# Attention order planned per engine, its output kept turned, w_o prepared early, and head loads moved to GpSimd's queue

## The reference

```
h = rms(x, g_pre_mix);  z = h @ w_in  -> q | k | v | f | B | C | u
logit(t, s) = q_t.k_s/8 + sum_{s<j<=t} log sigmoid(f_j + b_f),  s <= t;  attn = softmax(logit) @ v
conv = B * causal_conv3(C * u)
mix  = concat(rms(attn, g_attn_out), rms(conv, g_conv_out)) @ w_o
x    = x + rms(mix, g_post_mix)
y    = x + rms(relu(rms(x, g_pre_mlp) @ w_up)^2 @ w_down, g_post_mlp)
```

## Time and profile before

| | us |
|---|---|
| median of 3 runs (lowest, highest) | 2739.94 (2737.48, 2744.5) |
| the profiled execution's own time | 2737.44 |
| its span | 2735.8 |

### The profile page before, as it was taken

One profiled execution on the slowest core, in us unless ns is written; L12 is line 12 of the kernel. 1 busy time (PEld: TensorE's weight loads), 2 busy tenths in 40 slices (PEclk: granted clock), 3 DMA queues, 4 the chain that ended last, 5 costly groups with the idle time before them and its releaser, 6 DMA issues.

```text
span 2735.8 us, 41595 instructions
## 1 busy us (share of the span) xinstructions
PE 2664.9 (97%) x14966; PEld 2405.3 (88%) x14966; DVE 1515.6 (55%) x2603; ACT 1126.6 (41%) x2099; POOL 1300.7 (48%) x884
## 2 busy tenths in 40 slices
PE   8999999998999999999999999899999999999997
PEld 8999999897888888888889989889999988999996
DVE  5233344247888887765344344665556564556554
ACT  3201301107777877555333332534333344333433
POOL 3233334220101006553477776766556677566654
PEclk9999999999999999999999999999999999999999
DMA  6643534574565443568444546421211272212213
GB/s 199 199 123 110 175 108 142 189 199 103 124 150 122 100 102 117 167 183 244 143 168 163 196 169 225 170 74 64 77 61 61 85 277 96 73 61 66 72 61 108
DMA packets 294353, 364.26 MB, mean 133 GB/s; under 512 B 37576, under 2 KB 245392, under 8 KB 290128
## 3 DMA queue, kind: packets, MB, share of 16 engines
q1 hardware_dynamic: 257152, 316.15, 37.7%
q0 software_dynamic: 11808, 26.74, 3.1%
q10 hardware_dynamic: 25264, 19.66, 2.1%
HBM read 264.30 MB, written 97.94 MB: 132 GB/s over the span
## 4 chain that ended last, share of the span: by engine, by line
PE 46%; DVE 2%; POOL 1%; DMA 1%; issue 1%; ACT 0%; SPq 0%; DVEq 0%; POOLq 0%; ACTq 0%
PE dn_bank L3006 17%; PE up_bank L2982 15%; PE dn_bank L2962 7%; PE up_bank L2937 7%; DMA m_raw_up<-in_w_up 1%; DVE m_raw_up L2758 1%; POOL m_y L2517 1%; POOL m_w_up L2466 1%; DVE m_t L2758 0%; SPq L2342 0%; ACT m_junk L2659 0%; DVE m_y L2863 0%; DMA m_x<-scratch_x 0%; POOL m_u L2509 0%; DVE m_y L2817 0%
## 5 line engine op out<-in xcount | busy, mean ns | idle before, releaser
L3006 PE MATMUL dn_bank<-m_w_dn,m_u 128*128 128x512 f32 x2304 | 531.0, 391 | 5.4 <-ACT m_y L2692 4.3
L3006 PEld LDWEIGHTS dn_bank<-m_w_dn,m_u 128*128 128x128 f32 x2304 | 432.7, 188 | 96.0 <-ACT m_y L2692 4.0
L2982 PE MATMUL up_bank<-m_h,m_w_up 128*128 128x384 f32 x2688 | 476.1, 337 | 8.7 <-DVE m_stage L2772 4.5
L2982 PEld LDWEIGHTS up_bank<-m_h,m_w_up 128*128 128x128 f32 x2688 | 470.1, 189 | 12.7 <-issue 5.1
L2819 DVE TENSOR_TENSOR m_y<-dn_bank,m_y 128x1024 f32<-128x1024 f32 x168 | 205.7, 1224 | 270.4 <-PE dn_bank L3006 270.4
L508 POOL TENSOR_TENSOR w_lo<-w_raw,w_hi 128x1024 fp32r<-128x1024 f32 x72 | 176.0, 2448 | 342.3 <-DVE w_hi L722 342.3
L2509 POOL TENSOR_TENSOR m_u<-m_stage,m_u 128x384 fp32r<-128x384 f32 x128 | 141.5, 1128 | 281.7 <-ACT m_u L2648 281.7
L2466 POOL TENSOR_TENSOR m_w_up<-m_raw_up,m_w_up 128x512 fp32r<-128x512 f32 x128 | 192.2, 1521 | 65.2 <-ACT m_w_up L2616 65.2
L938 PE MATMUL proj<-ha_hi,w_hi 128*128 128x384 f32 (+1 forms) x640 | 212.1, 331 | 0.0
L1446 DVE TENSOR_TENSOR p_lo<-t_bank,p_hi 128x512 fp32r<-128x512 f32 (+1 forms) x336 | 197.9, 599 | 25.2 <-ACT p_hi L1393 24.6
L938 PE MATMUL proj<-ha_hi,w_lo 128*128 128x384 f32 (+1 forms) x640 | 210.0, 328 | 0.0
(11 more groups left out here) (304 smaller groups left out, 5674.4 us busy)
## 6 DMA issues: line engine op xcount, KB each, us to landing
m_raw_up<-in_w_up SPq DMA_DIRECT2D x48, 1024.0 KB, 5.4
m_raw_dn<-in_w_down SPq DMA_DIRECT2D x47, 1024.0 KB, 4.9
w_raw<-in_w_in SPq DMA_DIRECT2D x72, 512.0 KB, 4.1
scratch_h_pairs<-m_pieces POOLq DMA_DIRECT2D x12, 1792.0 KB, 8.2
m_h<-scratch_h_pairs SPq DMA_DIRECT2D x14, 1536.0 KB, 10.8
nck<-scratch_ncum SPq DMA_DIRECT2D x8, 1312.0 KB, 19.2
scratch_v_hl<-vhl SPq DMA_DIRECT2D x20, 512.0 KB, 2.7
q_hi<-scratch_q_hi SPq DMA_DIRECT2D x16, 528.0 KB, 7.3
```

The lines of the kernel that those rows point to most:

```text
L2982: mm = pe.matmul(out, w_up[:, j, wp, k, :], hidden_rows(g, j, hp, k), start=(k == 0 and p == 0), stop=(k == KH - 1 and p == 2))
L3006: mm = pe.matmul(bank[:, cols], part, wd[:, wp, b, cols], start=(b == 0 and p == 0), stop=(b == 1 and p == len(passes) - 1))
```

## The change

- **Order.** `attention_steps` lists the steps of all 40 groups (8 heads; order 0, EXTRA, 1, 2, 3). `attention_order` plays them through with a cost and a delay for each step and gives every engine a queue of its own, unrolled. Among steps that could start at the same time TensorE prefers T, then S, then V; VectorE T, S; ScalarE T, M, O. The plan knows the waits among TensorE, VectorE and ScalarE (banks, score sets, p buffers). It has no DMA in it and no GpSimd.
- **Turned output.** Step N, `n_bank` and the output's transposes go; there are two `o_bank`. ScalarE copies the two halves of the bank to the same 64 partitions (two instructions), GpSimd adds them (64x512) and multiplies with `scales`. SyncE stores to `attn_t`, which keeps queries in columns. There are two `o_t` buffers (`A_BUFS` = 2), and ScalarE's copy of group k waits for the store of group k-2.
- **Totals.** `scales` needs the reciprocals along the columns. VectorE, before the first `p_lo` of a group, takes the reciprocal and transposes a [128, 32] tile in 32x32 blocks; SyncE stores it in four small DMAs (two for EXTRA) to `rtotal`, waits for them, and loads the line back, broadcast to 64 partitions.
- **w_o.** Eight pieces of 128 rows, one every third group from group 5 on: SyncE loads the piece, GpSimd scales it by the gain, rounds it, takes the rest, SyncE stores both to DRAM. The gains are no longer applied to a and c. After the products of head 6, GpSimd's queue loads `w_hi` and `w_lo` (8 MB).
- **Loads.** The ten loads of a head stand on GpSimd's queue, behind the close of group 3 of head h-2 and ahead of the close of group 0 of head h-1.
- **Mix.** a comes turned, so `scale_rows`, `turn` and VectorE's part of the split go. ScalarE copies a and c to hi (`firsts`), GpSimd squares and sums both and makes both rests; two 1-column matmuls.

```diff
+    def cost(engine, x):
+        if engine == "pe":
+            if x.kind == "S":
+                return 2 * (x.width / 2.4 + 13) + (107 if x.last else 0), 320
+            if x.kind == "T":
+                return 109 * (x.width // P), 260
+            return (2 * len(x.blocks) * 107 if x.group.extra else 2 * (x.width / 2.4 + 13)), 300
+        if engine == "dve":
+            return x.width / 0.96 + 67 + (400 if x.kind == "T" and x.first else 0), 150
...
+    while True:
+        chosen = None
+        for engine, kinds in FIRST_CHOICE.items():
+            for rank, kind in enumerate(kinds):
...
+                    start = max(free[engine], ready(engine, x))
+                    if start < math.inf and (chosen is None or start < chosen[0] or (start == chosen[0] and engine == chosen[1] and rank < chosen[2])):
+                        chosen = start, engine, rank, x
...
         def _(sp):
+            for q in groups:
...
+                store_scales(q)
+                load_scales(q)
+                k, at = divmod(q.k - W_FIRST, W_EVERY)
+                if 0 <= k < KB and at == 0:
+                    load_piece(k)
+                if 0 <= k < KB and at == 2:
+                    store_piece(k)
+                if q.k:
+                    store(groups[q.k - 1])
...
         def _(pool):
+            fetch(1)
+            for q in groups:
...
+                close(q)
+                k, at = divmod(q.k - W_FIRST, W_EVERY)
+                if 0 <= k < KB and at == 1:
+                    split_piece(k)
+                if q.g == GROUP_ORDER[-1] and q.head + 2 <= HEADS:
+                    fetch(q.head + 2)
...
         def _(act):
+                if x is last_turns[13]:
+                    front.firsts(act, 0, 0)
...
+                else:
+                    act.wait_ge(used, P_BUFS + q.products[-1].at + 1)
+                    if q.k >= A_BUFS:
+                        act.wait_ge(att_stored[q.k % A_BUFS], 16 * (q.k // A_BUFS))
+                    bank = o_bank[q.k % O_BANKS]
+                    act.activation(o_t[0:HD, q.k % A_BUFS, 0, 0:q.wide], bank[0:HD, 0:q.wide], ACT.Copy)
+                    act.activation(o_t[0:HD, q.k % A_BUFS, 1, 0:q.wide], bank[HD:P, 0:q.wide], ACT.Copy).then_inc(o_taken, 1)
...
         def _(dve):
+                    if x.first:
+                        dve.wait_ge(exp_done, q.maxima[-1].at + 1)
+                        dve.reciprocal(rtotal[:, q.k % 2, 0:q.n], total[:, sums(q)]).then_inc(recip_made, 1)
...
+                        dve.transpose(rtotal_t[:, q.k % 2, :], rtotal[:, q.k % 2, :]).then_inc(recip_done, 1)
...
-            def turn(t, s):
-                for j in range(CJ):
-                    tr = pe.transpose(t_bank[:, j * P:(j + 1) * P], ag[:, j * P:(j + 1) * P], ident[:, :])
...
-                pe.matmul(q_bank[:, 0:1], csq_one[:, :], ones[:, :], start=True, stop=True).then_inc(S["c_summed"], 1)
+                pe.matmul(q_bank[:, 0:1], square_sums[:, 0, :], ones[:, :], start=True, stop=True)
+                pe.matmul(q_bank[:, 1:2], square_sums[:, 1, :], ones[:, :], start=True, stop=True).then_inc(S["rows_summed"], 1)
```

More of the change, by code:

```diff
@@ new lines, with __init__ @@
+EXTRA = QT // 4
+GROUP_ORDER = (0, EXTRA, 1, 2, 3)
+W_FIRST, W_EVERY = 5, 3
+FIRST_CHOICE = {"pe": "TSV", "dve": "TS", "act": "TMO"}
+class Group:
+    def __init__(self, k, head, g):
+        self.k, self.head, self.g, self.par = k, head, g, head % 2
+        self.extra = g == EXTRA
+        self.tiles = [QT] if self.extra else list(range(4 * g, 4 * g + 4))
+        self.n = len(self.tiles)
+        self.rows = slice(SEQ, ROWS) if self.extra else slice(4 * g * P, 4 * g * P + 4 * P)
+        self.wide = P if self.extra else 512
+        self.set = 0 if self.extra else g % 2
+        self.before = None
+        self.stores = 0
+        self.scores, self.maxima, self.turns, self.products, self.out = [], [], [], [], None
@@ L1095, in attention_order @@
[L1095 to L1111, removed]
-            else:
[L1113 to L1144, removed]
-    before = scores(0, 0, 0)
-    body, late = [], None
[L1148 to L1154, removed]
-                parts += steps
-                late = Step("N", par, par, g=q, o=steps[-1])
-            if g == 0:
-                body.append(Step("L", 1 - par, par + 1))
-            body += mix(parts, scores(par, par, g + 1) if g + 1 < extra else scores(1 - par, par + 1, 0))
-    body.append(late)
-    def group_of(tile):
-        return extra if tile == QT else tile // 4
-    count = dict.fromkeys("LSMTVON", 0)
-    turned_by = {}
-    exps_by = {}
-    for x in before + body:
-        kind = x.kind
-        if x is body[0]:
-            start = dict(count)
-            turned_by[1] = count["T"]
-        x.at = count[kind]
-        count[kind] += 1
-        if x.kind == "M":
-            x.last_piece = count["S"] - 1
-            exps_by[x.off, group_of(x.tile)] = count["M"]
-        if x.kind == "S" and x.n == 0 and x.tile % 4 == 0 and x.tile < QT:
-            x.free = turned_by.get((x.tile // 4) % 2)
-        if x.kind == "T":
-            x.exps = exps_by[x.off, x.g]
-            turned_by[0 if x.g == extra else x.g % 2] = count["T"]
-    per = {k: count[k] - start[k] for k in count}
-    return before, body, start, per
@@ L1417, in _ @@
+            for x in queues["act"]:
+                step(x)
         @block.vector
@@ L1502, in step @@
                     mm.then_inc(used, 1)
-                elif x.kind == "N" and not (x is last_n and it == AGAIN):
-                    pe.wait_ge(o_taken, O_BANKS + upto("N", it, x.at) + 1)
-                    pe.wait_ge(n_taken, upto("N", it, x.at) + 1)
-                    for i in range(4 if x.g < EXTRA else 1):
-                        mm = pe.transpose(n_bank[:, i * P:(i + 1) * P], o_t[:, x.at % 2, i * P:(i + 1) * P], ident[:, :])
-                    mm.then_inc(in_rows, 1)
-            loop(pe, "pe", step)
@@ L1671, in mix_rows @@
         h2_lo = front.tile("h2_lo", [P, 2, KB, P], F32R)
[L1672 removed]
+        q_bank = early.banks()[1]
         c_bank = ctx.enter_context(nc.psum_tensor("c_bank", [P, D], F32))
```

695 lines of the change are left out of this document (336 added, 359 removed).

## The result

The changed kernel takes **2826.07 us** (median of 4 runs, 2825.11 to 2829.61), the kernel before 2738.78 beside it: ratio 1.0317, 95% interval 1.0299 to 1.0335. It is slower by 87 us; 2705 was forecast, with a range up to 2746.

A forecast was written before the change was run, and what follows sets the result against it. TensorE was taken as the bound, busy 2664.9 of 2735.8 us. Terms: transposes -15, order -23, loads and stores +8, mix -6, between stages +1.5, sum -34.5; forecast 2705 us, 8-in-10 range 2680 to 2746.

The forecast's parts named there:

- SyncE's store, 3.2 us to land, to 18: At a head's end: the store of group 0's output lands 18 us after group 3's last V.
- the stall of 1 us: ScalarE's copy of group 1, due at about 17 us, waits 1 us for that store at each of six boundaries.
- 6 (due at 12): Upper bound for the stall per boundary: 6 us if ScalarE's copy is due at 12 us, against 0 if at 22.9.
- the upper end of 51: Attention's stalls for loads and stores: 8 us added, with ends 0 and 51.
- C: Rival, attention: the ten loads hold GpSimd's queue, 14 us wait at each of six boundaries, 2785 us; chance 0.12.
- D: Rival, attention: stores partly not hidden, copies due at 12 and splits in the way, 51 instead of 8, 2748 us; chance 0.10.
- over 30 us speaks for D or C: Sign in attention: ScalarE idle before the o_t copy for DMAs, a few us a head expected; over 30 in all favours D or C.
- I take 2: Three w_o pieces split beside head boundaries, ahead of a close: 0 to 15 us added, 2 taken.
- Order and transposes: Attention on TensorE: removing step N's transposes saves 15 us; the new order, filling gaps between groups, saves 23 us.
- VectorE's transpose below 0.3 us: Sign in attention: each of VectorE's 40 transposes of [128, 32] takes under 0.3 us; priced at 0.17, hidden.
- 0.07: Mix stage: the added 1-column matmul costs TensorE 0.07 us a tile, against 0.43 saved by dropping the turn; 6 us off.
- The MLP is untouched: The MLP stage, after the mix: no change in time, so no term in the sum.

The follow-up runs named there:

- the fastest run: Changed kernel with four output buffers, gains in attention's own tile (old addresses) and w_o pieces split away from the heads' ends: 2703.11 us, ratio 0.9878.

## Why the prediction was wrong

By profiled spans the 87.7 us are made up so: two buffers cost 91.9 (2795.3 against 2703.4); the shifted addresses 21.6 (2730.7 against 2709.1); the splits at the heads' ends 5.7 (2709.1 against 2703.4); all the rest gains 32.4 (2703.4 against 2735.8). The sum is +86.8. The parts come from different pairs of kernels, so it could have been some us off without being wrong. One part can be read twice: addresses and splits cost 27.3 together with four buffers, and 28.2 with two (2823.5 against 2795.3).

**The step that failed** is "SyncE's store, 3.2 us to land, to 18" and the stall of 1 us that followed. For the head shown the path was followed rightly, and every other time in it was near. The ten issues took 6.1 us for 9.3, so the store went out at 12.7 and not at 14.7; the copy was due at 15.8, for 17. But 3.2 was the median of a line's stores over a whole stage, and this store is always issued into the burst of ten loads that the same walk had just put there. It took 10.9 us here, and 15.7 at the longest. The price of the stall was 1 us at each of six boundaries; by the eight waits there it is 14.9. The bound "6 (due at 12)" varied the due time, which was right, and never the landing, which was wrong; so the upper end of 51 was no end. With what was measured the same walk gives 12.7 + 10.9 - 15.8 = 7.8 us for this head, and the trace has 7.87. At the other boundaries stores that go out late, behind a piece's stores or the totals, come on top; the walk had both as hidden or at 2 us. Over all ten waits it is 97.9. The clock falls as well: the granted clock of the window 622 to 1076 is 0.89, where the fastest run has 0.99. The 92 us between runs with and without the waits hold both; the clock's share alone wasn't measured.

Its rivals: *C* had the right sign and the nearest time (2785, still 41 us short) for a wrong reason. GpSimd's queue isn't held (ten issues in 6.1 us); the DMA engines are full (share 1.00 from 700 to 720). *D* had the right wait, as the text said ("over 30 us speaks for D or C"), with too small a price. The prediction cited the Trainium skill (DMA: Bandwidth & Descriptors, Issuing engines are not separate DMA queues) for what moving the loads would not gain. The trace agrees, and more than was drawn from it: the store on SyncE's queue and the loads on GpSimd's shared the engines, and 128 KB took 10.9 us. The same page (SWDGE vs HWDGE vs iDMA) says that each DMA engine goes round between its internal queues; by that one would expect a small transfer to slip past a long queue of another, and here it did so poorly: 10.2 to 15.8 us behind a burst, 3.8 at the median of all.

**w_o.** Its price was 4.4 us a piece; it is 6.3 by the changed kernel's trace (2.84, 1.04 and 2.40), for the scaling was set equal to the rounding's 1.0 and took 2.84. "I take 2" for the three splits is 5.7 by the runs with four buffers, within the 0 to 15. How they cost there was other than said: not a close held back, but the next head's loads held back, and in the other order the totals' stores. The 16 MB more through the DMA engines were taken as harmless; no run tests that by itself.

**Order and transposes** had the right sign and about half the size. With four buffers and the pieces moved, attention ends 20.5 us earlier (first product of c_bank at 1064.0 for 1084.5). The forecast had 28.5 (15 + 23 - 8 - 1.5), and its 8 us of stalls are gone in this kernel, so 36.5 is what 20.5 must be held against. Group-3 copies are 53.8 us apart, where 52.7 came from the sum. Before, the seven periods from 683.64 to the last such copy, at 1084.29, are 57.2 us on average, not quite the 57.5 of the first two. So they save 3.5 each, 24.3 in all, and the first copy of group 3 comes 3.8 later (687.46 for 683.64). If step N's 1.9 a head is right, the order gave 1.6 a head and not 2.9. "VectorE's transpose below 0.3 us": 0.21, nothing to be seen of it.

**Mix.** -6 was forecast and -3.7 came, once the operands stood as before (from the first to the last product of c_bank, 207.6 for 211.3). The turn is gone, but the second 1-column matmul costs more than "0.07". Changed kernel, TensorE, answering to the earlier trace rows:

```profile
1211.55 0.28 PE L1933 MATMUL up_bank<-mix_ones,mix_square_sums 128*128 128x1 f32 x2
1211.69 0.36 PE L1934 MATMUL up_bank<-mix_ones,mix_square_sums 128*128 128x1 f32 x2
1211.91 0.47 PE L1942 MATMUL c_bank<-wo_hi,c_hi 128*128 128x512 f32 x1
```

From 1211.55 to 1211.91 it is 0.36 for 0.14 before, so 0.43 - 0.22 = 0.21 a tile, 3.6 in all. In the kernel as changed the addresses took even that away.

**"The MLP is untouched"** was the second wrong step, and nothing in the argument looked at it: no line of it was edited, but its tiles moved. Once they were back, the MLP was 8.2 us *shorter* than before (2703.4 - 1271.6 against 2735.8 - 1295.8). No edit explains that. The traces show where 6.4 of it lie: between the first and the last matmul of the long down group (976.6 us before, 970.2 after), where TensorE had waited 5.4 us ahead of its matmuls, 4.3 of them for ScalarE's `m_y`, and now waits 0.9. Where both have the shifted tiles, the kernel before with 32 bytes (1449.3) and four buffers alone (1447.3) differ by 2.0 only, so most of it may belong to the one execution that was profiled of the kernel before; why ScalarE was late there is open. So the 2703 so close to the forecast is partly luck: attention gave 8 us less than the sum said, although its 8 us of stalls were gone, and the MLP 8 more.

## What to carry to other kernels

When a wait hangs on a transfer, take its landing from the moment at which it is issued, not from the median of its line: look for what else is in the DMA engines then, and if it is a burst, price it by the maximum. Give small hand-over buffers (outputs, totals) enough of them to outlast the burst; two more here were worth 92 us, and three weren't tried. After adding a tile, compare the durations of matmuls in stages that weren't edited; put new small tiles behind the others, or see to it that the two operands of the long matmul groups still start at the same place modulo 256.

## What the runs showed of the hardware

- A TensorE matmul with 128x512 moving and 128x128 stationary f32 data depends on where its two tiles start relative to each other. With nothing but 32 bytes of shift, 389 ns turn into 395 for nearly all of 2304 matmuls, and the kernel goes from 2734 to 2752 us. By the addresses in the program (bytes in a partition, modulo 256): at the same place it is 389 ns, be it at 128 (`m_w_dn` at 66176 and `m_u` at 125568; `wo_hi` at 17024 and `a_hi` at 97408), at 160 or at 0 (`m_w_dn2` at 84128 and `m_u` at 125600; 84224 and 125696). With 32 bytes between them it is 395, with 64 it is 394 (`m_w_dn_even` at 192320 and `m_u` at 125568, in the kernel before), with 128 it is 393. That fits all groups looked at. No group had exactly 256 bytes between the two, so the period may be 512; what lies behind it wasn't tried. The Trainium skill (SBUF — State Buffer, Operand start alignment) asks only for a multiple of the element size and says that its rule is about legality, not speed; here addresses that obey it differ in speed.
- The stores of attention's outputs (128 KB) land in 3.8 us at the median and in up to 15.7 behind ten loads of another queue; four stores of 0.5 KB took 13.
- GpSimd issues loads with 2048 rows of 512 bytes in 1.19 us, where the same load held SyncE's queue for 17.39. The loads land no sooner for it (24.0 us for the values at the median, 20.9 in the kernel before).
